# Sixteen more tokens through gathered expert rows instead of the dense product: 336 columns and 84 gate groups per layer

## What is computed

```
q = xn @ w_q                       # 8 heads, two halves of 128
s1, s2 = scores of 128 sub-keys for each half; top 16 of each
top 16 of the sums -> ids (i1*128 + i2), g = softmax(top scores)
act = sum_d u[ids] * xn            # u, v: 16384 x 1024
y = sum_heads sum_16 g * gelu(act) * v[ids]
```

## Time and profile before

| | |
|---|---|
| median of 3 runs | 3249.09 us (3245.47 to 3250.68) |
| the profiled execution | 3244.68 us |
| its span, first to last instruction | 3242.9 us |
| PE busy | 3218.6 us |
| DVE busy | 2567.0 us |
| ACT, POOL busy | 1502.4, 1100.5 us |
| bytes moved by DMA | 874.95 MB, mean 270 GB/s |

### The profile page before, as it was taken

How to read it: one execution, slowest core, us unless ns; L and a number is a source line. 1 busy time by engine, 2 the same in 40 slices (tenths; PEclk the granted TensorE clock), 3 DMA queues, 4 the chain that set the end, 5 groups by cost and what they waited for, 6 DMA issues and landing times.

```text
span 3242.9 us, 54568 instructions
## 1 busy us (share of the span) xinstructions
PE 3218.6 (99%) x19718; PEld 3033.2 (94%) x19718; DVE 2567.0 (79%) x4932; ACT 1502.4 (46%) x2310; POOL 1100.5 (34%) x713
## 2 busy tenths in 40 slices
PE   8999999999999999999999999999999999999998
PEld 8878888999999999999988788889999999999998
DVE  6654449999998889999866544499999888899997
ACT  5553233367773333333355532333777733333333
POOL 1000014334337455555300000143333365555552
PEclk9999999999999999999999999999999999999999
DMA  4214322589999999999721143225999999999996
GB/s 148 78 53 143 141 88 91 190 320 381 381 383 408 353 363 387 410 407 402 300 92 66 54 155 130 98 100 180 345 379 380 379 414 350 370 389 407 413 413 251
DMA packets 226059, 874.95 MB, mean 270 GB/s; under 512 B 22240, under 2 KB 67440, under 8 KB 178016
## 3 DMA queue, kind: packets, MB, share of 16 engines
q1 hardware_dynamic: 112912, 455.25, 37.3%
q0 software_dynamic: 93008, 337.91, 26.8%
q10 hardware_dynamic: 19968, 79.65, 6.1%
HBM read 791.33 MB, written 81.40 MB: 269 GB/s over the span
## 4 chain that ended last, share of the span: by engine, by line
PE 99%; DVE 1%; issue 0%; ACT 0%; DMA 0%; ACTq 0%; DVEq 0%
PE bank L1449 30%; PE bank L1451 29%; PE bank L1450 29%; PE bank L1758 5%; PE bank L1567 1%; PE bank L1604 1%; PE bank L1585 1%; PE bank L1708 1%; PE bank L1549 1%; PE bank L1477 0%; PE bank L1857 0%; DMA h<-in_x 0%; DVE lg L1074 0%; PE bank L1572 0%; PE bank L1865 0%
## 5 line engine op out<-in xcount | busy, mean ns | idle before, releaser
L583 ACT ACTIVATE hi<-raw 128x2048 fp32r<-128x2048 f32 (+2 forms) x338 | 620.2, 1835 | 765.3 <-PE bank L1451 731.8
L1449 PE MATMUL bank<-xT_hi,hi 128*128 128x352 f32 (+1 forms) x2688 | 925.7, 344 | 1.9 <-DVE xT_lo L986 1.7
L1450 PE MATMUL bank<-xT_lo,hi 128*128 128x352 f32 (+1 forms) x2688 | 910.5, 339 | 0.0
L1451 PE MATMUL bank<-xT_hi,lo 128*128 128x352 f32 (+1 forms) x2688 | 909.9, 339 | 0.0
L936 DVE TENSOR_TENSOR lo<-raw,hi 128x2048 fp32r<-128x2048 f32 (+2 forms) x320 | 699.4, 2186 | 247.1 <-ACT hi L583 244.9
L1449 PE MATMUL bank<-w_hi,hi 128*128 128x352 f32 x2048 | 660.2, 322 | 0.0
L1451 PE MATMUL bank<-w_hi,lo 128*128 128x352 f32 x2048 | 658.7, 322 | 0.0
L1450 PE MATMUL bank<-w_lo,hi 128*128 128x352 f32 x2048 | 657.2, 321 | 0.0
L1449 PEld LDWEIGHTS bank<-xT_hi,hi 128*128 128x128 f32 x2688 | 505.7, 188 | 31.9 <-issue 5.7
L1451 PEld LDWEIGHTS bank<-xT_hi,lo 128*128 128x128 f32 x2688 | 505.7, 188 | 25.7
L572 POOL DMA_INDIRECT rows<-in_v_rows,ids x256 | 417.3, 1630 | 327.1 <-DVE h L1327 271.8
(11 more groups left out here) (237 smaller groups left out, 3989.4 us busy)
## 6 DMA issues: line engine op xcount, KB each, us to landing
raw<-in_stream SPq DMA_DIRECT2D x352, 1024.0 KB, 7.0
gate_in<-gate_d SPq DMA_DIRECT2D x96, 384.0 KB, 11.2
act_d<-act_s ACTq DMA_DIRECT2D x92, 352.0 KB, 6.2
gate_d<-gate_s ACTq DMA_DIRECT2D x22, 1472.0 KB, 9.7
act_in<-act_d SPq DMA_DIRECT2D x92, 352.0 KB, 9.3
gate_d<-gate_s ACTq DMA_DIRECT2D x22, 576.0 KB, 14.1
gate_in<-gate_d SPq DMA_DIRECT2D x32, 256.0 KB, 7.9
rows<-in_u_rows,ids POOLq DMA_INDIRECT x256, 8.6
```

Source lines behind the costliest of these rows:

```text
L583: act.activation(hi[s][:, 0:n], raw[s][:, 0:n], ACT.Copy).then_inc(hi_done, 1)
L1449: pe.matmul(dst, a_[0], b_[0], start=first, stop=False)
L1450: pe.matmul(dst, a_[0], b_[1], start=False, stop=False)
L1451: return pe.matmul(dst, a_[1], b_[0], start=False, stop=last)
```

## The change

A third group of `F` = 16 tokens (80 to 95 of tile 2) leaves the dense way, which keeps `TM` = 336 tokens. The products, the copies of ids and gates, and the turn back use 336 columns. `GROUPS` becomes 84, so `G_STEPS` 28 with `G_SHORT` 0, and the rounds begin at position 42 with 22 U chunks. The buffers of activations, weights and gates keep 352 columns, and so do their transfers and the ACT and DVE instructions on them.

Each of the 16 tokens is spread over `KF` = 8 partitions with 16 experts each, so 16 gathers for U and 16 for V (`ROW_OPS` 352). Since the tokens don't begin on a quarter of the partitions, their ids, gates and x rows are spread by way of three small DRAM tensors: 3 stores from POOL before row operation 7, and 2 + 8 loads before row operation 40. A second matrix `spread_f` is loaded by POOL late in the layer and adds two fp32 matmuls at its end. DVE gets three small instructions behind the ids, one product for `x_f`, and one small multiply; ACT one 64-partition DMA issue and one small GELU.

```diff
+F = 16
+TM = TU - F
+KF = P // F
-GROUPS = TU // G_TOK
+GROUPS = TM // G_TOK
-ROW_OPS = 2 * (E + P)
-U_ROW_OPS = E + P
+F_OUT, F_IN, F_SPREAD = 7, 40, 240
+ROW_OPS = 2 * (E + P + F)
+U_ROW_OPS = E + P + F
...
+                    if n == F_OUT:
+                        wait_alone(pool, f_found, l + 1, pool_passed)
+                        for dst, src in (f_ids_d, act_row[F_ROWS_OF].bitcast(U32)), (f_g_d, w_row[F_ROWS_OF]):
+                            pool.dma_start(dst.rearrange("q t k -> t q k"),
+                                           src.rearrange("t (q k) -> t q k", q=KF)).then_inc(f_out, 16)
+                        wait_alone(pool, f_scaled, l + 1, pool_passed)
+                        pool.dma_start(f_x_d, x_f[F_ROWS_OF]).then_inc(f_x_out, 16)
+                    if n == F_IN:
+                        wait_alone(pool, f_out, 32 * (l + 1), pool_passed)
+                        for dst, src in (ids_f, f_ids_d), (g_f, f_g_d):
+                            pool.dma_start(dst, src.rearrange("q t k -> (q t) k")).then_inc(f_in, 16)
+                        wait_alone(pool, f_x_out, 16 * (l + 1), pool_passed)
+                        for kf in range(KF):
+                            pool.dma_start(x_f[kf * F:(kf + 1) * F], f_x_d).then_inc(f_x_in, 16)
+                    if n == F_SPREAD:
+                        wait_alone(pool, g_ps, GROUPS * (l + 1) + G_RING, pool_passed)
+                        pool.dma_start(spread_f[:], a["spread_f"]).then_inc(f_spread, 16)
...
+                extra(dve.scalar_tensor_tensor(out=w_row[F_FROM], in0=idx_t[F_FROM, E_TILE, 0], scalar=P,
+                                               in1=idx_t[F_FROM, E_TILE, 1], op0=ALU.mult, op1=ALU.add))
+                extra(dve.tensor_scalar(act_row[F_FROM].bitcast(U32), w_row[F_FROM], P * P * l, None, ALU.add))
+                dve.tensor_copy(w_row[F_FROM], g_t[F_FROM, E_TILE]).then_inc(f_found, 1)
...
-                        last = product(ps[i][:, 0:TU], at(w, i * NK + kk), at(xT, kk, slice(0, TU)), kk == 0, kk == NK - 1)
+                        last = product(ps[i][:, 0:TM], at(w, i * NK + kk), at(xT, kk, slice(0, TM)), kk == 0, kk == NK - 1)
...
-                            done = product(ps[d][:, 0:TU], at(v, i * NK + d), at((w_hi, w_lo), s, i),
+                            done = product(ps[d][:, 0:TM], at(v, i * NK + d), at((w_hi, w_lo), s, i, slice(0, TM)),
...
-                        pe.wait_ge(row_done, ROW_OPS * l + U_ROW_OPS + E)
+                        pe.wait_ge(row_done, ROW_OPS * l + U_ROW_OPS + E + F)
+                        pe.wait_ge(f_spread, 16 * (l + 1))
-                            pe.matmul(ps[2 * NDT + nh][:], spread[:], y_e[:, nh * T:(nh + 1) * T], start=True, stop=True)
+                            pe.matmul(ps[2 * NDT + nh][:], spread[:], y_e[:, nh * T:(nh + 1) * T], start=True, stop=False)
+                            pe.matmul(ps[2 * NDT + nh][:], spread_f[:], y_f[:, nh * T:(nh + 1) * T], start=False, stop=True)
```

More of the change, by code:

```diff
@@ L128, in by_act @@
 def by_act(st, b):
-    return 2 * st + b - G_SHORT + 1
+    return 2 * st + b - max(G_SHORT, 1) + 1
 HALVED = range(2, 9)
@@ L163, with row_of @@
 DOWN_OF = {down_at(c): c for c in range(C_V)}
+def row_of(n):
+    if n < U_ROW_OPS:
+        return ("e", n) if n < E else ("row", n - E) if n < E + P else ("f", n - E - P)
+    n -= U_ROW_OPS
+    return ("e", n) if n < E else ("f", n - E) if n < E + F else ("row", n - E - F)
 def rows_by(q):
@@ L349, in build @@
         start.close()
-        idx1T, idx2T = sb("idx1T", [P, TD]), sb("idx2T", [P, TD])
-        gT = sb("gT", [P, TD])
+        idx1T, idx2T = sb("idx1T", [P, TU]), sb("idx2T", [P, TU])
+        gT = sb("gT", [P, TU])
         act_s = sb("act_s", [P, 2, 2, TU])
+        ids_f, act_f, g_f, w_f = (x[:, 0:F] for x in (mx, nmx, esink, rden))
+        ids_f = ids_f.bitcast(U32)
+        x_f = y_f = sb("x_f", [P, D])
         x_row = sb("x_row", [P, D])
@@ L421, in build @@
         v_ps, yT_act, yT_dve = sem("v_ps"), sem("yT_act"), sem("yT_dve")
+        f_found, f_out, f_in, f_scaled, f_x_out, f_x_in, f_spread = (
+            sem(n) for n in ("f_found", "f_out", "f_in", "f_scaled", "f_x_out", "f_x_in", "f_spread"))
         round_ps, round_ev = sem("round_ps"), sem("round_ev")
@@ L829, in _ @@
                         act.dma_start(x_e[E_ROWS], a["norm_rows"][l, E_ROWS]).then_inc(norm_e_in, 16)
+                        act.dma_start(x_f[F_FROM], a["norm_rows"][l, F_FROM]).then_inc(norm_e_in, 16)
                         act.activation(g_t[:], g_t[:], ACT.Exp).then_inc(exp_ready, 1)
@@ L852, in store_gates @@
                 def store_gates(w):
-                    act.wait_ge(g_ev, l * GROUPS + (w + 1) * PER_SLICE + G_RING)
+                    act.wait_ge(g_ev, l * GROUPS + min((w + 1) * PER_SLICE, GROUPS) + G_RING)
                     first = P - KEPT_ROWS
@@ L888, in _ @@
                             store_act(j, s)
-                        if q >= 0 and q % PER_SLICE == PER_SLICE - 1:
+                        if q >= 0 and (q % PER_SLICE == PER_SLICE - 1 or q == GROUPS - 1):
                             store_gates(q // PER_SLICE)
@@ L903, in _ @@
                         act.wait_ge(row_done, ROW_OPS * l + U_ROW_OPS)
+                        act.activation(w_f, act_f, ACT.Gelu)
                         act.activation(w_row[:], act_row[:], ACT.Gelu).then_inc(row_gelu, 1)
@@ L1289, in _ @@
                 quarter = lambda kq: slice(kq * E, (kq + 1) * E)
-                extra = Chain(dve, e_link, 5 * l, 5)
+                extra = Chain(dve, e_link, 7 * l, 7)
                 for kq in range(KQ):
@@ L1307, in row_op @@
                 def row_op(n):
-                    N, k = ROW_OPS * l + n, (n % U_ROW_OPS - E) % P
+                    N, (of, k) = ROW_OPS * l + n, row_of(n)
+                    first = k == 0
                     k = slice(k, k + 1)
                     row = rows[:, N % NR]
-                    dve.wait_ge(rows_in[N % NR], 16 * (N // NR + 1))
[L1313 to L1318, removed]
+                    if n == E:
+                        dve.wait_ge(f_out, 32 * (l + 1))
+                    if n == E + P:
+                        dve.wait_ge(f_in, 32 * (l + 1))
+                        dve.wait_ge(f_x_in, 16 * KF * (l + 1))
+                    dve.wait_ge(rows_in[N % NR], 16 * (N // NR + 1))
+                    if n < U_ROW_OPS:
+                        x_, dots = {"e": (x_e, act_e), "row": (x_row[:], act_row), "f": (x_f[:], act_f)}[of]
+                        last = dve.tensor_tensor_reduce(row, row, x_, 1.0, 0.0, ALU.mult, ALU.add, dots[:, k])
+                    else:
                         dve.wait_ge(row_done, ROW_OPS * l + n)
@@ L1321, in row_op @@
                             dve.wait_ge(e_weighed, l + 1)
-                            last = dve.tensor_scalar(y_e, row, w_e[:, k], None, ALU.mult)
-                        else:
[L1324 to L1328, removed]
+                        y_, w_ = {"e": (y_e, w_e), "row": (h[:, ROWED], w_row), "f": (y_f[:], w_f)}[of]
+                        if of != "row" and first:
+                            last = dve.tensor_scalar(y_, row, w_[:, k], None, ALU.mult)
+                        else:
+                            last = dve.scalar_tensor_tensor(out=y_, in0=row, scalar=w_[:, k], in1=y_, op0=ALU.mult, op1=ALU.add)
                     last.then_inc(row_done, 1)
@@ L1357, in _ @@
                 assert rows_by(ROW_GELU_AT - 1) >= U_ROW_OPS and rows_by(WEIGH_ROWS_AT - 1) <= U_ROW_OPS + E
+                assert F_IN < E + P and F_SPREAD > U_ROW_OPS
                 def round_sums(r):
```

36 lines of the change are left out of this document (26 added, 10 removed).

## The result

The changed kernel is a little slower: 3253.36 us against 3246.29 us (medians of 20 runs each), ratio 1.0017 with the 95% interval 1.0010 to 1.0023 (the two medians alone give 1.0022). I forecast 3225 us.

The account below looks back on a forecast made before the run. PE sets the pace now, with DMA a close second limit and DVE third. Terms +9.9, +7.3, -25.1, -3.7 and +1.7 sum to -9.9 us a layer, -19.8 for two, from 3244.68 to 3225 us; range 3184 to 3264.

Parts of the forecast that it names:

- the gate steps: Gate-step stretch, 28 steps after the change: 284 us forecast for 309.1, -25.1 us a layer, bounds -28.3 and -21.
- find: Search stretch of 14 positions, where DVE must end before PE's transposes: -3.7 us a layer, bounds -4.5 and -2.
- One of the signs: V stretch: PE, now never idle, would wait for `lo`, about 0.5 us a position.
- Rival 1: All stretches: PE and DVE keep the pace, DMA takes the rest; -39 us a layer, 3167 us, chance 0.11.
- Rival 3: Gate steps: DVE is late, a step stays at 10.35 us; +6 us a layer, 3237 us, chance 0.05.
- the V term: V stretch, 46 positions, DMA last: 363.7 us against 353.8, +9.9 a layer, bounds -1.9 and +16.9.
- the term of the rounds: Rounds, 40 positions after 38, at 122.1 MB: 299.5 us against 292.2, +7.3 a layer, bounds +2.6 and +18.5.
- The check over all: Gate steps, rounds and V stretch together: 379.1 MB in 947.2 us, 400 GB/s; worth nothing at 396.
- rival 4: Little or no change, DMA at 394 to 398 GB/s over the three stretches, 3238 to 3251 us, chance 0.11.
- rival 2: Rounds and V stretch: DMA stays below 396 GB/s, DVE's waits delay `lo`; +17.5 us a layer, 3280 us, chance 0.23.
- The sign that I gave for rival 2: V stretch staying under 400 GB/s, at DMA share 1.03 or below 1.00.

Follow-up runs that it names:

- run 5: Changed kernel, every second row gather of the V stretch replaced by a 64-bytes-a-partition load, VectorE's passes kept full: 3209.45 us, 0.9882 of the kernel before.
- run 6: Changed kernel, every second row operation of the V stretch cut to 16 of 1024 columns on VectorE, all gathers kept: 3254.49 us, 1.0023.
- run 9: Changed kernel, every second of U gathers 96 to 159 replaced by a 64-bytes-a-partition load, VectorE's passes kept full: 3225.51 us, 0.9933.
- run 10: Changed kernel, every second of U operations 96 to 159 cut to 16 of 1024 columns on VectorE, all gathers kept: 3251.62 us, 1.0016.
- run 3: Changed kernel with its products at 352 columns again, everything else kept: 3282.31 us, 1.0104 of the kernel before.
- run 7: Changed kernel, first eight parts of gate loads issued one each at positions 46 to 53 instead of bunched at 50 to 55: 3251.48 us, 1.0010.
- run 8: Changed kernel, the 14 row operations of positions 42 to 45 thinned to 3 and spread over the rest of the rounds: 3263.54 us, 1.0051.
- run 11: Changed kernel with gate loads one each at positions 46 to 53 and row operations placed by bytes, all computation kept: 3256.73 us, 1.0035.
- run 1: Changed kernel, the new tokens' 32 gathers a layer replaced by 64-bytes-a-partition loads, VectorE's passes kept full: 3245.99 us, 0.9986 of the kernel before.
- run 2: Changed kernel, VectorE's 32 passes a layer over the new tokens' rows cut to 16 of 1024 columns, all gathers kept: 3248.81 us, 0.9997.

## Why the prediction was wrong

*What held.* PE's saving per position (7.37 forecast, 7.4 found), the gate steps (284 and 283.5), find (-3.7 and -3.1), and the main claim, that DMA ends last in the V stretch. That it is bytes and not VectorE is shown by runs 5 and 6, and VectorE's own 7.45 by the first of them. That 7.94 us were found for 7.93 forecast is luck in part: between 1300 and 1600 us the engines gave 412 and not 407 GB/s, and a position carried 3.26 MB (123.70 MB over 1822 / 48 positions) and not 3.23. One of the signs was off: in the V stretch PE waits for `w_lo`, not for `lo`. Rival 1 is out: V positions took 7.94 us, and the fullest 7.4 us of the trace, from 2570.6 us on, have 424 GB/s and not the 438 that it needs. Rival 3 is out: gate steps take 10.1 us, with 280.46 of 283.5 us busy on VectorE. The byte count held over all: 379.3 MB in the three stretches of the windows above, 379.1 forecast. The lower bound of the V term was added up wrongly: 44 x 7.69 + 2 x 7.37 is 0.7 us under 353.8, not 1.9; nothing hangs on it.

*The step that failed* is the term of the rounds, +7.3 us, measured +22.5 in the profiled execution and about +20 by the mean of the six layers, outside its own upper bound of +18.5. The text set two ceilings for them, 393 GB/s (the mean of now, scaled by its share to 1.03) and the 412 to 420 of the best 20 to 50 us, and chose near the second "since the lower end is nearer". The windows show 392 GB/s over 314.9 us. So the rate to plan with was the scaled mean, 310.7 us, and a busiest stretch of 50 us is not what 300 us of the rounds can hold. Runs 9 and 10 show that the two large stalls were bytes.

Most of the last 4 us above 310.7 are bytes too: the rounds carried 123.4 MB and not 122.1, 3.3 us at 392 GB/s, while the gate steps carried 111.4 and not 113.9.

The scaled mean is right by its number rather than by its sum, since the share came to 1.00 and not 1.03. Nor is 392 shown to be what the engines can do: the rounds have 407 GB/s in their first 59 us, where the longest stall lies, and 380 at a share of 0.97 between 1048 and 1136 us, where PE waits only for the 1.9 us at position 63. The excess comes where demand is over the engines' rate, and what they have free later doesn't pay it back. What the clock costs in net was not measured apart; the three positions of 9.0 us behind the stalls are 4.8 us over PE's pace.

For the V stretch a rate over 300 us could have been read before. The second layer of the kernel before, which I didn't cut, has it, with PE never waiting:

```profile
2894.00:3194.00 300.00, 300.00 (x1890) 300.00 (x1889) 276.95 (x221) 104.70 (x80) 166.69 (x103) 1.00 1.03 411
```

*The check over all was right and its rate was wrong.* It said that 396 GB/s over the three stretches is the point where the change is worth nothing, and 2.4 us a layer for each GB/s. Measured: 379.3 MB in 962.4 us, 394 GB/s, which by the same rule is +5 us a layer. The layers show +4.6 (1068.5 against 1063.9) and +7.4. The second layer of the kernel before is 4 us shorter than its first, mostly at V positions of 7.63 us where the first has 7.68; no run explains that, and the forecast counted both layers alike. With 400 I was 6 GB/s too high, 1.5%, and this alone turns -20 us into +9. The case that came is the lowest edge of my rival 4, with rival 2's mechanism at the place that it names; rival 2's price came from 389, too low. Rival 4's own times don't fit its rates: by my sum 394 GB/s is 3255 us, not 3251. The sign that I gave for rival 2 was near as well: the whole V stretch has 397 GB/s at share 0.99. A forecast whose sign hangs on 1% of a rate should have had much less than 0.64 on one side.

*The rule of the pages.* The Trainium skill, DMA: Bandwidth & Descriptors, Where 436 GB/s comes from, gives 435 GB/s as the ceiling of the ports that the 16 engines use. The trace agrees with it as a ceiling for stretches of 7 us and more: 424 in the fullest 7.4 us, 412 over 300 us in the V stretch, 392 and 393 in the rounds and gate steps. Single slices of 1.5 us in the DMA views read up to 447. As a rate to plan with it is too high here: these mixes stayed 5 to 10% below it.

*Where the gain went.* PE's columns give back 81 us only where DMA has time. In find and the gate steps they did (-3.1 and -25.6 a layer, part of the latter two steps fewer, which come back as two more positions). In the other 646 us a layer the kernel before had a DMA share of 0.97 to 0.98 with PE waiting once, for 0.4 us. There PE saves about 86 x 0.32 = 28 us, and by my estimate each new row operation takes about 1.3 us of all 16 engines (0.524 MB at 400 GB/s), 42 us for the 32. Run 3 measured what the narrower products are worth in the rounds and the V stretch of the kernel after: nothing within the spread of executions.

## What to carry to other kernels

A chain that is 99% one engine doesn't say that the others have room: read the DMA share by stretch, and where it stands at 0.97 or above, a change that trades PE time for bytes has to be priced at the bytes. Take for each stretch its own mean, scaled to a share near 1.03, as the rate that it can hold, not the best 50 us: here that gives 395, 393 and 409 GB/s for gate steps, rounds and V stretch, and 393, 392 and 397 came (412 between 1300 and 1600 us of the V stretch). When demand passes that rate, moving transfers around may only move the stall, as in runs 7, 8 and 11: work out demand over capacity for each place first, for all engines and not only for the one that was looked at.

An experiment that takes one cost away has to take it away where the wait is. Runs 1 and 2 removed the new work, but the schedule had put it elsewhere.

## What the runs showed of the hardware that I had not expected

- The DMA share alone doesn't give the rate: the rounds of before have 374 GB/s at 0.98 and those of after 392 at 1.00, the V stretch 412 at 1.03. Queue q0, which has gathers of 4 KB rows alone, gave 25.5 GB/s an engine in the V stretch (57.13 MB in 46.7% of 16 x 300 us) and 24.8 between 1048 and 1136 us of the rounds (19.37 MB in 55.5% of 16 x 88 us), 3% less with packets of the same size; why was not tested:

```profile
DMA packets 8556, 33.43 MB, mean 380 GB/s; under 512 B 840, under 2 KB 2299, under 8 KB 7027
...
q0 software_dynamic: 5319, 19.37, 55.5%
q1 hardware_dynamic: 3232, 13.98, 41.3%
```

- A stall of PE costs more than its length. After waits of 6.95, 4.83, 1.91 and 1.89 us in layer 1 the granted clock was at its lower level, 1.2 GHz, for a few us (a mean of 0.77 in the first stall, 0.75 in the 7 us behind it, 0.51 in the 3.5 us behind the wait of 1.91 us). Matmuls of 336 columns started 0.28 us apart instead of 0.154, and the next position took 9.0 us instead of 7.4. The 19 waits between 1300 and 1600 us, 1.7 us at most, left the clock at 1.00.
